# The second norm's factors as a row through memory, in a fused two-block kernel on one core

## The reference, cut to what matters

```python
def rmsnorm(x, g):
    x32 = x.astype(jnp.float32)
    y = x32 * lax.rsqrt(jnp.mean(x32 * x32, axis=-1, keepdims=True) + EPS)
    return y.astype(x.dtype) * g

x = x + jnp.einsum('bse,ed->bsd', mix, w_out[l])
h2 = rmsnorm(x, norm2_g[l])
gate = jnp.einsum('bsd,df->bsf', h2, w_gate[l])      # D_FF = 2816
up = jnp.einsum('bsd,df->bsf', h2, w_up[l])
x = x + jnp.einsum('bsf,fd->bsd', jax.nn.silu(gate) * up, w_down[l])
return rmsnorm(x, final_norm_g)
```

## Time and profile before

| | us |
|---|---|
| median of 3 runs | 3658.86 |
| lowest, highest | 3658.35, 3659.91 |
| the profiled execution: its own time | 3659.9 |
| its span (first to last instruction) | 3658.2 |
| TensorE busy | 3622.5 |
| VectorE busy | 2040.5 |
| ScalarE busy | 1509.4 |
| GpSimd busy | 688.7 |

### The profile page before, as it was taken

The page is one execution under the profiler, slowest core; times in us unless marked ns, Lnnn a source line. Parts: engine busy times, 40 slices in busy tenths (PEclk is TensorE's granted clock), DMA queues, the critical chain, the costliest instruction groups (busy, mean ns, idle before and its releaser), DMA issues. The chain is left out here.

```text
span 3658.2 us, 62817 instructions
## 1 busy us (share of the span) xinstructions
PE 3622.5 (99%) x25608; PEld 3126.7 (85%) x25608; DVE 2040.5 (56%) x3852; ACT 1509.4 (41%) x2754; POOL 688.7 (19%) x408
## 2 busy tenths in 40 slices
PE   9999999999999999999999999999999999999999
PEld 7889888978897988987788878888877899998998
DVE  5667635551645354457655675555566565546555
ACT  4332431231232363566655665444555422223222
POOL 3001130000000000233333321000000244415442
PEclk9999999999999999999999999999999999999999
DMA  8756687557655877876776665544542666666664
GB/s 309 269 198 248 237 302 253 203 205 244 219 220 191 285 249 240 296 240 215 257 232 209 231 232 193 176 158 154 170 150 107 228 253 245 234 239 232 233 235 184
DMA packets 215822, 820.57 MB, mean 224 GB/s; under 512 B 22128, under 2 KB 71536, under 8 KB 152432
## 3 DMA queue, kind: packets, MB, share of 16 engines
q1 hardware_dynamic: 215536, 816.57, 63.4%
HBM read 615.15 MB, written 201.33 MB: 223 GB/s over the span
## 5 line engine op out<-in xcount | busy, mean ns | idle before, releaser
L1713 PE MATMUL bank<-slot,Z0b 128*128 128x512 f32 (+1 forms) x3504 | 703.6, 351 | 2.3 <-DVE R L2594 2.3
L1713 PEld LDWEIGHTS bank<-slot,Z0b 128*128 128x128 f32 x3504 | 559.7, 188 | 92.9 <-DVE R L2594 4.0
L1713 PE MATMUL bank<-Z1b,slot 128*128 128x512 f32 (+1 forms) x2568 | 605.5, 379 | 1.8 <-DVE Z1b L2641 1.1
L1713 PE MATMUL bank<-Z1a,slot 128*128 128x512 f32 (+1 forms) x2568 | 602.9, 378 | 1.4 <-DVE Z1a L2536 1.2
L1713 PEld LDWEIGHTS bank<-Z1b,slot 128*128 128x128 f32 x2568 | 445.2, 189 | 90.5 <-issue 5.0
L1713 PEld LDWEIGHTS bank<-Z1a,slot 128*128 128x128 f32 x2568 | 444.2, 188 | 88.9 <-issue 3.3
L3217 POOL TENSOR_TENSOR slot<-raw,slot 128x1024 fp32r<-128x1024 f32 x111 | 275.8, 2493 | 691.4 <-ACT slot L2222 691.4
L2594 DVE SCALAR_TENSOR_TENSOR R<-bank,small,R 128x512 f32<-128x512 f32 x352 | 261.2, 747 | 173.2 <-PE bank L1713 172.8
L2947 DVE TENSOR_SCALAR_CACHE_REDUCE P<-bank 128x512 f32<-128x512 f32 (+3 forms) x320 | 189.0, 608 | 228.7 <-PE bank L1713 228.0
L3235 POOL TENSOR_TENSOR Z0b<-AF,Z0b 128x512 fp32r<-128x512 f32 x88 | 134.4, 1527 | 783.6 <-ACT Z0b L2421 783.6
L1713 PE MATMUL bank<-KS,DQ 128*128 128x512 f32 (+3 forms) x960 | 276.1, 388 | 5.5 <-DVE P L2947 2.0
(11 more groups left out here) (271 smaller groups left out, 5510.4 us busy)
## 6 DMA issues: line engine op xcount, KB each, us to landing
slot<-Wd SPq DMA_DIRECT2D x350, 1024.0 KB, 5.5
Wd<-slot SPq DMA_DIRECT2D x130, 1024.0 KB, 7.6
raw<-in_wts_dram SPq DMA_DIRECT2D x209, 512.0 KB, 4.6
DQ<-Qd SPq DMA_DIRECT2D x192, 128.0 KB, 3.9
slot<-Wd SPq DMA_DIRECT2D x40, 512.0 KB, 6.4
DV<-Vd SPq DMA_DIRECT2D x60, 256.0 KB, 4.9
KS<-Kd SPq DMA_DIRECT2D x24, 512.0 KB, 7.1
KS<-Kd SPq DMA_DIRECT2D x24, 384.0 KB, 7.0
```

The lines of the kernel that those rows point to most:

```text
L1713: return e.matmul(o, a, b, start=start, stop=stop, skip_group_check=True)
```

## The change

Four things are changed. The product with ones, the scaled unit matrices and the copy go. Instead SyncE writes the 4 factors of each partition to a small array `Fd` in device memory, waits for it to land, and reads it back as one row for all partitions. In the planner the root now stands behind the evacuation of the last transposed rows (T2, k = 7). And the gate's first evacuation waits for the read to land. Costs of the planner follow, so the order of other instructions moves too.

```diff
@@ Order.norm2 (the planner's lane)
         for p in range(2):
             yield ("ev", ("E", s, 3, p))
         yield max(P.end[("ev", ("E", s, 3, p))] for p in range(2))
-        t = P.put(("n2", s), ("dve", 150), ("act", 1500), ("dve", 1400))
-        yield t + 1000
-        yield from self.short(("rb", s), ("pe", 940), ("dve", 690), after=t)
+        yield ("ev", ("T2", s, 0, 7))
+        t = P.put(("n2", s), ("dve", 150), ("act", 1500), ("dve", 150))
+        yield t
+        t = self.dma(("rb out", s), 65536, t)
+        if s:
+            yield ("ev", ("Fg", s - 1, NF - 1))
+        t = self.dma(("rb in", s), 262144, t)
+        yield t
+        P.put(("rb", s))
@@ Order.phase_f
-                yield from self.fm(("Fg", s, b), t, 1, zr, ("dve", 690), ("act", 610), behind=() if b else (("ev", ("rb", s)),))
+                yield from self.fm(("Fg", s, b), t, 1, zr, ("dve", 690), ("act", 610), behind=() if b else (("rb", s),))
...
@@ TensorE
-            def factor_rows(s):
-                bank_free(("rb", s))
-                pe.wait_ge(*pool_c("one"))
-                pe.wait_ge(*dve_n2("n2", s, "d"))
-                mm(bank_of("rb", s)[:, :], lamp[:, :, :].rearrange("p a n -> p (a n)"), GS[0][:, :], True, True).then_inc(
-                    *pe_rb.inc("rb", s))
@@ VectorE, gate
                 dve.wait_ge(*pe_g("ev", label))
-                dve.wait_ge(*dve_n2("rb", s))
+                dve.wait_ge(*d_fi("rb in", s))
+                if n == 0:
+                    if s:
+                        dve.wait_ge(*act_ln("ln", s - 1, NT - 1, "sq"))
+                    else:
+                        dve.wait_ge(*pool_pl("pl halo", S - 1))
@@ VectorE, factor_rows and norm2
-                e.tensor_copy(factors, bank_of("rb", s)[:, :]).then_inc(*dve_n2.inc("rb", s))
...
-                for c in range(NT):
-                    x = e.tensor_scalar(GS[0][:, tok(c)], ident, r2[:, c:c + 1], None, ALU.mult)
-                x.then_inc(*dve_n2.inc("n2", s, "d"))
@@ SyncE
+            def factors_out(s):
+                sp.wait_ge(*dve_n2("n2", s, "r"))
+                if (v := d_fo.at["rb out", s] - d_fo.whole) > 0:
+                    sp.wait_ge(d_fo.sem, v)
+                e.dma_start(Fd[s].rearrange("(c p) -> p c", p=128), n2_r2[s % 2], allow_slow_non_contiguous=True).then_inc(
+                    *d_fo.inc("rb out", s))
+
+            def factors_in(s):
+
+                sp.wait_ge(*d_fo("rb out", s))
+                if s:
+                    sp.wait_ge(*dve_g("ev", ("Fg", s - 1, NF - 1)))
+                else:
+                    sp.wait_ge(*act_c("masks"))
+                    sp.wait_ge(*dve_c("lam1"))
+                transfer(factors, Fd[s].partition_broadcast(128), d_fi, "rb in", s)
```

More of the change, by code:

```diff
@@ L987, in phase_f @@
                     yield from self.fm_two([("Fg", s, 0), ("Fu", s, 0)], t, 1, zr, [[("dve", 690), ("act", 610)], [("dve", 690)]],
-                                           [[("ev", ("rb", s))], [("ev", ("Fg", s, 0))]])
+                                           [[("rb", s)], [("ev", ("Fg", s, 0))]])
                     P.add(self.split_act(s, b), True)
@@ L1268, in build @@
         X1d = dram("X1d", [T, D])
+        Fd = dram("Fd", [S, SUB])
         Y2d = dram("Y2d", [S, 4, 128, 2, SUB])
@@ L1385, in build @@
         pe_sc = signal("pe_score", of("sc"))
-        pe_rb = signal("pe_factors", of("rb"))
         pe_tr = signal("pe_transposed", plan.tp_uses)
@@ L1454, in build @@
         dve_n2 = signal("dve_norm2", [x for st in order for x in (
-            [st + (y,) for y in ("ss", "r", "d")] if st[0] == "n2" else [st] if st[0] == "rb" else [])])
+            [st + (y,) for y in ("ss", "r")] if st[0] == "n2" else [])])
         dve_ts = signal("dve_token_sums", of("tl"))
@@ L1481, in build @@
         d_r = landed("d_r", of("r in"))
+        d_fo, d_fi = landed("d_factors_out", of("rb out")), landed("d_factors", of("rb in"))
         d_Y = {}
@@ L1515, in evacuated @@
                 return act_pl(*label)
-            if label[0] == "rb":
-                return dve_n2(*label)
             return act_g("ev", label) if by_act(label) else dve_g("ev", label)
@@ L2057, in tensor @@
                     finish_stick(*a)
-                elif kind == "rb":
-                    factor_rows(*a)
         def scalar(e):
@@ L3026, in finish_stick @@
                     *dve_fin.inc("fs c", i, c, "y"))
-            def factor_rows(s):
-                dve.wait_ge(*pe_rb("rb", s))
-                if s:
-                    dve.wait_ge(*dve_g("ev", ("Fg", s - 1, NF - 1)))
-                else:
-                    dve.wait_ge(*act_c("masks"))
-                e.tensor_copy(factors, bank_of("rb", s)[:, :]).then_inc(*dve_n2.inc("rb", s))
             def norm2(s):
@@ L3043, in norm2 @@
                 e.reciprocal(r2, r2).then_inc(*dve_n2.inc("n2", s, "r"))
-                dve.wait_ge(*dve_n2("n2", s, "r"))
-                if s:
-                    dve.wait_ge(*act_ln("ln", s - 1, NT - 1, "sq"))
-                    dve.wait_ge(*dve_g("ev", ("Fu", s - 1, NF - 2)))
-                else:
-                    dve.wait_ge(*pool_pl("pl halo", S - 1))
-                for c in range(NT):
-                    x = e.tensor_scalar(GS[0][:, tok(c)], ident, r2[:, c:c + 1], None, ALU.mult)
-                x.then_inc(*dve_n2.inc("n2", s, "d"))
             def last_factor(s, c):
@@ L3249, in gpsimd @@
                     pool.wait_ge(*dve_c("lam1"))
-                    e.memset(lamp[:, :, :], 1.0)
                     e.memset(P1[:, 2048:2049], 1.0).then_inc(*pool_c.inc("one"))
@@ L3466, in sync @@
                     transfer(gf[:, :], rows[:, 2 * D:3 * D], d_c["gf"], "gf")
+                elif kind == "rb out":
+                    factors_out(*a)
+                elif kind == "rb in":
+                    factors_in(*a)
                 elif kind == "x1 in":
```

## The result

The changed kernel takes 3678.98 us (median of 5 runs, 3675.84 to 3683.05), the kernel before 3659.53 in the same comparison (3658.35 to 3661.46). The ratio is 1.0050, interval 1.0039 to 1.0061: slower, by 19.5 us, where 2.9 us less were forecast. The third rival ("the factors are late", 3678) is what happened.

The account below looks back on a forecast made before the run. TensorE bounds the kernel, busy 3622.5 of 3658.2 us. Piece 0 +1.3, piece 1 -2.7, pieces 2 and 3 -1.5, DMA pair zero: -2.9 from 3658.9 gives 3656.0 us, range 3648 to 3666.

Parts of the forecast that it names:

- The third rival: Factors late: write and read take so long that VectorE stands at the gate's evacuation and TensorE stops; 22 us, 3678, chance 0.09.
- The DMA pair: Write and read of the factors on SyncE land before the gate's evacuation is due; taken as zero, bounds 0 and +20.
- three signs: Forecast wrong if VectorE idles for the DMA into `pvt`, the write alone exceeds 6 us, or TensorE's waits move over 7 us.
- The bound of +20: Slow bound in us of the write and read of the factors, assigned to the third rival, chance 0.09.
- SyncE: Queue behind the write and read: loads of weights, queries and keys, none due within 5 us.
- Piece 1: Between last transposes and the gate's next matmuls: 3.4 us shrinks to 0.7 of waiting, 2.7 won; bounds 3.4 and 0.9.
- Piece 0: Around the first factors: 2.8 us won before the scores, 3.4 lost in later waits, 0.7 for clock; +1.3, bounds -4.3 to +5.
- The two later waits: Piece 0, behind the scores: TensorE waits 2.0 us on ScalarE's transposed probabilities, then 1.4 us on VectorE's score bank.
- half a loss: Piece 0, behind the single 3.2 us wait: half the earlier half-clock loss of 2.9 us was counted, 1.5 us.
- Pieces 2 and 3, -1.5 us: TensorE restarts sooner behind the seven-product part's sum; -0.75 us each, bounds -0.86 to +1.0 per piece.
- The second rival: Order worse: replanned attention gives pieces 0 and 1 further waits of 2 to 3 us and half clock; +8, 3664, chance 0.13.

Follow-up runs that it names:

- old order with 16 bytes: Kernel before, every engine's order kept: product removed, factors through memory in 16-byte pieces, row copied once per piece with a step; 3660.9 us, ratio 1.0002.
- the old order: Kernel before, every engine's order kept, no replanning: scaled matrices, product and copy removed, single-element write and read put on SyncE; 3674.6 us, ratio 1.0037.
- the last run: From the old order with 16 bytes: row by memory only in pieces 0 and 1, root moved behind last transposed rows; 3661.6 us, ratio 0.9999.

## Why the prediction was wrong, step by step

**The DMA pair: the step that failed.** I took zero for it, with the write going out behind a weights load and the pair landing "near 1616" in piece 0. I had priced 2 KB by its size, and the shortest landing that I called like it is of 256 KB; besides that I had only the queue in front. Measured, the write alone takes 12.4, 11.3, 8.6 and 7.0 us from issue to landing in the four pieces, and 9.0 on idle queues. From its issue to the evacuation it is some 16 us in piece 0 (1613.32 to 1629.36), and TensorE waits 16.1 us in pieces 0 and 1, where the third rival counted 13. In pieces 2 and 3 that rival counted 9.4 and TensorE lost 2.7 against the run with 16-byte pieces (27.6 and 25.7 us from the last transposes to the sum's restart, against 25.3): there the token sums covered the pair, as the main text said. To this comes half clock behind the waits: TensorE's busy time is 2.5 us above that of the run with 16-byte pieces. So the rival's mechanism is what happened, but that its 3678 is so near 3679.0 is luck in part: it counted too much for pieces 2 and 3, too little for 0 and 1, and nothing for the clock. Changing only the write's pattern to pieces of 16 bytes gives back all 19 us; 64 bytes between the elements does so too, with the read's source changed beside it. All three signs that I had named for a wrong forecast were there: VectorE waited for the DMA into `pvt`, the write took over 6 us, and TensorE's idle time moved by over 7 us.

The bound of +20 stood in the text, but its chance of 0.09 had no row behind it. "It is only 2 KB" was no evidence: no row had its form. The Trainium skill, page "DMA: Bandwidth & Descriptors", section "Rules for kernel authors", spoke for the slow end. The runs agree with its advice against a non-contiguous last dimension, but not with a price by the element: 512 elements 64 bytes apart take 1.9 us. The same page, section "Specifications", says that a transfer under 512 B is done as a read, a change and a write. That holds for pieces of 16 bytes and of 4 alike, so it doesn't tell 1.4 us from 9.0; whether elements side by side wait for each other's write there is not shown.

**SyncE.** I said that nothing queued behind the pair is due within 5 us. SyncE was held up to 12.5 us, but in the changed kernel the loads behind it cost little (1.0 us for `slot<-Wd`). What I missed is that transfers issued beside the write land late.

**Piece 1.** Of its 3.4 us, 0.7 was to be left as a wait; the trace has 0.27. The step was right, and the 7.66 us behind it hid the gain.

**Piece 0.** The first wait was to be 3.2 us, and is 3.08. The two later waits (2.0 for `TP`, 1.4 for `P`) are 0.91 and 0.60. For the clock behind the first wait I took half a loss, 1.5 us. The profiled execution of the changed kernel has none (granted clock 1.00 from 1600 to 1606), but this differs between executions of one order: from the restart behind the 3.08 us to the next scores it is 7.5 us there, and 9.0 in the run with 16-byte pieces (granted clock 0.72 from 1601 to 1607). From the end of the scores to the next it is 10.5 us in the one and 12.1 in the other, against 15.0 before and 12.2 forecast. With the two later waits this part would have been -3.0 or -1.4 us, and not +1.3, had the factors come in time.

**Pieces 2 and 3, -1.5 us.** Right, but for the late factors. In the run with 16-byte pieces each wins 1.0 us where I had 0.75, and the gate's evacuation starts at 2925.10, 15.65 us behind the last transposes, which is 2922.6 in the time of the kernel before; I had put 2923. In the changed kernel itself piece 2 loses 1.3 us and piece 3 wins 0.6. In the old order with 16 bytes the gain isn't there: 27.0 and 26.8 us, the product's absence being given back in waits for `pu`. So the gain comes with the new order, which has the root behind the last transposed rows and the token sums ahead of the gate's evacuation; which of the two it takes isn't shown.

**The order.** The second rival had half its mechanism: the replanned attention has a wait of 5.6 us and half clock at 1739, which stays with a fast write. With the savings above it comes out even (3659.9). I had no row for this wait, and it takes away what pieces 1, 2 and 3 win. So, against before: single elements cost 13.5 us in the old order, 19 in the new one. With a fast write the change can't be told from none, in either order.

## What to carry to other kernels

Price a small transfer by the form of its pieces at the memory side, not by its bytes: look for a row of that form, and where there is none, the forecast must lean on the slow bound, or the transfer be measured alone. The numbers of one partition go to memory as one piece, side by side, and the order of the row is mended by one copy on the chip. Removing work from the busiest engine wins only if what releases its next step comes earlier as well. And two profiles are two executions: before a difference of spans is explained, find a run of the same order and see where the two part.

## What the runs showed of the hardware

- 4-byte elements written side by side to memory: 512 in 9.0 and 8.0 us, 128 in 7.2 and 6.7, on idle queues. The same 512 64 bytes apart: 1.9 and 2.2. 128 pieces of 16 bytes: 1.4. The time lies behind the packets: from the last packet to the landing 7.6 us for 512 elements side by side and 6.2 for 128, against 0.6 and 0.3 for the other two forms. Reading 512 single elements that lie side by side: 2.1 in both passes.
- Such a write holds back others: a 256 KB read issued 0.5 us behind it landed after 11.4 us, against 5.2; a 512 KB load issued 0.4 us ahead of it after 11.1, against 4.6 and 4.8 with the other two forms.
- TensorE's clock behind a wait of 3.08 us in one and the same order: granted 1.00 in one execution, 0.72 over 6 us in another.
- VectorE multiplying 128x512 4-byte values with one operand read at a step of 16 bytes takes 1071 ns for 682. This agrees with the Trainium skill, page "SBUF — State Buffer", section "Door 1: The DMA port swizzle", by which each access that crosses to a new line of 16 bytes pays a penalty; it gives no size. A copy of 128x512 values with that step took 0.62 us in the last run, less than the 0.69 of the copy from a bank before, so the penalty doesn't show there.
